# Three fp32r products in place of one fp32 matmul in the attention scores and logits of a hybrid decoder block

## The chip, the cores and the metric

The kernel runs on one core of a Trainium2 chip. A core has a matmul engine (TensorE, PE in the profile, with its weight loads as PEld), VectorE (DVE), ScalarE (ACT), GpSimd (POOL) and SyncE (SP), each with its own instruction queue that is worked off in order, and 16 DMA engines. The metric is device microseconds of one execution; the median of three runs is compared.

## The reference

The block takes x of 512 tokens by 1024 channels in float32. Two branches run in parallel on a normalised h, and an MLP follows.

- `h = rms_norm(x) * (1 + scale1) + shift1`, where scale and shift are products of `silu(c)` with `w_ada`.
- Attention branch: `q_lat` is projected to 8 heads of 64 (`a_q`) and to 4 index heads of 64 (`q_idx`). An index score `sum_h w_idx * relu(q_idx . k_idx)` is made for each query and key; each query keeps the 128 best causal keys, and softmax attention runs over these.
- Recurrent branch: HGRN2, a gated linear recurrence over 4 heads of 128, computed in levels of doubling blocks.
- Both are merged by sigmoid gates, projected and added to x; then a second norm, `square(relu(h2 @ w_mlp1))`, and `w_mlp2`.

The index scores decide which keys are kept, so they are computed with float32 accuracy.

## The kernel before

Everything is transposed, with channels on the 128 partitions and tokens along the free axis. The kernel is one program per engine, written out by hand; engines meet at named semaphores only. Almost all large products are made as three matmuls in fp32r, a float32 format that the array takes in one pass: an operand is split into a `hi` part (a copy to fp32r, made on ScalarE by `split_hi` and its like) and a `lo` part (the float32 value minus `hi`, made on VectorE or GpSimd), and `hi*hi + hi*lo + lo*hi` is summed in PSUM. A plain float32 matmul stands in the trace as two instructions.

The order of work on TensorE is:

1. Start. `x_square` puts squares of x into `x_sq` on ScalarE (seven of eight slices); VectorE (`x_add`) adds them in pairs; TensorE sums four 128x128 blocks of each pair against `ones` into bank 7 (L1650). ScalarE takes the root (`XRS`, L551), VectorE its reciprocal (L1046), and TensorE spreads it over the partitions (`row_spread`). `idle_products(n)` are matmuls whose result nobody reads. VectorE also makes the modulation vector with one dot product of 1024 columns for each slice (`ada_dot1`, L1027).
2. The first projection, `a_pass` (L1662): for each of 8 slices of h, 7 units times three products.
3. The latent q: `lat_hi`, `lat_lo`, the sum of its squares, the index key norm (`KRS`, L588, spread at L1631) and `q_idx` (L1693 to L1695), then v (`values_step`) with the index scores in between: `scores(qb)` at L1731, plain float32, for query blocks 1 to 3 of 128 tokens with 256, 384 and 512 keys. Two heads share a 128-partition tile, so each is a matmul of 64 rows.
4. VectorE finds the 128 best keys by 16 rounds of max-8 and replace; TensorE goes on with the projections of the recurrent branch, and the recurrence itself follows.
5. Attention over four pairs of heads p = 0 to 3. `logits(p, 0, 4)` and `logits(p, 4, 8)` (L1976, plain float32) make 8 tiles of 512, 512, 384, 384, 256, 256, 128 and 128 keys; VectorE masks them (L1347), ScalarE takes the exponential (L804), VectorE divides by the sum (L1356), TensorE transposes (L1989), ScalarE copies the transposes to `prT` (L785), and `values(p)` (L2004) follows. `gate_blocks` of the merge gates fill TensorE's time in between; their results leave on ScalarE by `gate` (L764), and the next unit in the same bank waits for that.
6. The projections, the second norm, and the MLP in two halves: `up` (L1612 to L1614), ScalarE's `up_relu` (L886), `up_square` and `tforms_hi` (L899), and a Strassen-like `quads` (L2187 to L2189).

Of the kernel before, what the change touches and what calls it, by code (L numbers as in the profile page):

```python
# [22 lines left out]
P = 128  # L23
# [36 lines left out]
def hybrid_block(nc, xt, c, cols, ada_t, w_units, out):  # L60
# [17 lines left out]
    with ExitStack() as ctx:  # L78
# [25 lines left out]
        qT = place("qT", RA + 8 * KB, [P, AC, T])  # L104
        score = place("score", RA + 16 * KB, [P, TB, T])
# [14 lines left out]
        qiT = place("qiT", RL + 16 * KB, [P, RC, T])  # L120
# [13 lines left out]
        ada_drop2 = place("ada_drop2", RL + 10 * KB, [P, D])  # L134
# [12 lines left out]
        sig_b = place("sig_b", RL + 16 * KB, [P, KC, T])  # L147
        sq_o = place("sq_o", RA + 16 * KB, [P, 2, T])
# [52 lines left out]
        def sem(name):  # L201
# [13 lines left out]
        xsq_ready, xsq_added, xsq_summed, xroot_ready, xspread = (  # L215
            sem("xsq_ready"), sem("xsq_added"), sem("xsq_summed"), sem("xroot_ready"), sem("xspread"))
        a1_ready, xn_ready, hfull_ready = sem("a1_ready"), sem("xn_ready"), sem("hfull_ready")
        slice_done, a_done = sem("slice_done"), sem("a_done")
        lat_ready, latsq_ready, latsq_added = sem("lat_ready"), sem("latsq_ready"), sem("latsq_added")
        kw_ready, kwsq_ready, k_taken = sem("kw_ready"), sem("kwsq_ready"), sem("k_taken")  # L220
        ki_summed, ki_root, ki_spread, ki_ready = (sem("ki_summed"), sem("ki_root"), sem("ki_spread"),
# [77 lines left out]

        LOGIT_BANK = [[6, 4, 2, 3], [6, 7, 4, 5]]  # L300
# [206 lines left out]
        def _(act):  # L507
# [43 lines left out]
            nc.scalar.activation(XRS, bank[7][:, 0:T:P], ACT.Sqrt, scale=1.0 / D, bias=EPSC  # L551
# [21 lines left out]
            for k in range(RC):  # L573
                act.wait_ge(a_done, k + 1)
                nc.scalar.activation(lat_hi[:, k], bank[k][:], ACT.Identity,
                                     scale=col[:, V_QG + k:V_QG + k + 1])
                nc.scalar.activation(sq[:, k], bank[k][:], ACT.Square).then_inc(latsq_ready, 1)
# [3 lines left out]
            nc.scalar.activation(kw_sq[0:HD, :], bank[2][0:HD, :], ACT.Square).then_inc(kwsq_ready, 1)  # L581
            act.wait_ge(slice_done, 7)
# [8 lines left out]
            for m in range(2):  # L591
                act.wait_ge(qi_done, m + 1)
                nc.scalar.activation(qiT[:, m], bank[SCORE_BANK[m]][:], ACT.Copy).then_inc(qi_taken, 1)
# [4 lines left out]
            split_hi(U_V + 3)  # L598
            nc.scalar.activation(LBC, LBC, ACT.Exp)
# [385 lines left out]
        def _(dve):  # L985
# [14 lines left out]
            def x_add(p):  # L1000

                dve.wait_ge(xsq_ready, [2, 4, 5, 7][p])
                v.tensor_tensor(x_sq[:, 2 * p], x_sq[:, 2 * p], x_sq[:, 2 * p + 1], ALU.add).then_inc(xsq_added, 1)
# [7 lines left out]
            x_add(0)  # L1011
            c_product(0)
            x_add(1)
            c_product(1)
            dve.wait_ge(x_loaded[2], 16)
            step(v.tensor_tensor(x_sq[:, 5], xT[:, 5], xT[:, 5], ALU.mult))
            x_add(2)
            x_add(3)
# [44 lines left out]
            for k in range(RC):  # L1063
                dve.wait_ge(latsq_ready, k + 1)
# [3 lines left out]
            dve.wait_ge(t_lo, KC)  # L1068
            v.tensor_tensor(lat_sq[:], sq[:, 0], sq[:, 1], ALU.add).then_inc(latsq_added, 1)
# [4 lines left out]
            for r in (0, HD):  # L1074
                v.scalar_tensor_tensor(out=kiT[r:r + HD, :], in0=kw[0:HD, :], scalar=KIG, in1=bank[2][0:HD, :],
                                       op0=ALU.mult, op1=ALU.mult).then_inc(ki_ready, 1)
            dve.wait_ge(lat_root, 1)
# [4 lines left out]
                            LRS.unsqueeze(2).to_broadcast([P, TB, IH]), ALU.mult).then_inc(wi_ready, 1)  # L1082

# [228 lines left out]
            def ada_add(i):  # L1312
# [6 lines left out]
                v.tensor_tensor_reduce(out=ada_drop2[:], in0=src[:], in1=c_act[:], scale=1.0,  # L1319
# [4 lines left out]
            def oa_low(j):  # L1324
# [3 lines left out]
                                ALU.subtract).then_inc(oa_ready, 1)  # L1328

            dve.wait_ge(q_ready, 1)  # L1330
            for p in range(PAIRS + 1):
# [5 lines left out]
                if p < PAIRS:  # L1337
# [5 lines left out]
                    for t, qb, e in heads(p):  # L1343
# [6 lines left out]
                            accum_out=smx[:, 1, 2 * p + e, qb:qb + 1]).then_inc(logit_masked, 1)  # L1350
                    for t, qb, e in heads(p):
# [4 lines left out]
                        v.tensor_scalar(w, w, s, None, ALU.mult).then_inc(prob_ready, 1)  # L1356
                    if p == 0:
# [244 lines left out]
        def _(pe):  # L1602
# [53 lines left out]
            idle_products(5)  # L1656
# [33 lines left out]
            for m in range(2):  # L1690
                b = SCORE_BANK[m]
                for i, j in enumerate((m, 2 + m)):
# [30 lines left out]
            def scores(qb):  # L1723
                n = (qb + 1) * P
                for h in range(IH):
                    r = HD * (h % 2)
                    s = nscore[0]
                    nscore[0] += 1
                    if s >= IH:
                        pe.wait_ge(rel_ready, s - IH + 1)  # L1730
                    mm(bank[SCORE_BANK[h]][:, 0:n], qiT[r:r + HD, h // 2, qb * P:(qb + 1) * P], kiT[r:r + HD, 0:n],  # L1731
                       start=True, stop=True).then_inc(score_done, 1)
# [21 lines left out]
            pe.wait_ge(qi_taken, 2)  # L1754
            pe.wait_ge(ki_ready, 2)
# [208 lines left out]
            def logits(p, t0, t1):  # L1964

                for t, qb, e in heads(p)[t0:t1]:
                    i = 8 * p + t
# [298 lines left out]
```

## Time and profile before

| | |
|---|---|
| median of three runs | 771.15 us (770.37 to 771.26) |
| profiled execution, own time | 771.27 us |
| its span, first to last instruction | 769.4 us |
| TensorE busy in the span | 761.0 us (99%) |
| VectorE, ScalarE, GpSimd busy | 630.9, 364.7, 62.7 us |

An instruction's time in the trace includes its way through the engine, so neighbouring matmuls overlap. What a matmul costs a full TensorE is the distance from its start to the start of the next. The profiled execution is 0.12 us above the median.

### The profile page before, as it was taken

How to read it: one execution, taken by the hardware profiler on the slowest of the kernel's cores; microseconds unless marked ns; L12 is line 12 of the kernel's file. 1: busy time of each engine (PE TensorE's matmuls, PEld its weight loads, DVE VectorE, ACT ScalarE, POOL GpSimd, SP SyncE). 2: the span in 40 equal slices, each digit the busy share in tenths (PEclk: the TensorE clock that was granted, in tenths of full speed). 3: DMA queues.
4: the chain of work that ended last, by engine and by line, in shares of the span. 5: the costliest groups of instructions: out<-in, count | busy, mean ns of one | idle time of the engine just before them, and what ended most of it. 6: DMA issues, size and time to landing. Idle time of an engine off the chain costs nothing.

```text
span 769.4 us, 13224 instructions
## 1 busy us (share of the span) xinstructions
PE 761.0 (99%) x5208; PEld 645.8 (84%) x5208; DVE 630.9 (82%) x1129; ACT 364.7 (47%) x577; POOL 62.7 (8%) x64
## 2 busy tenths in 40 slices
PE   7999999999999999999999999999999999999998
PEld 6876878777878777778889988889999888889998
DVE  6975999778998677769966999879998766779996
ACT  5466524455344376654332555654333354454341
POOL 5015344200000000000012000000000000000000
PEclk9999999999999999999999999999999999999999
DMA  9943223221221233345556255312333433213331
GB/s 349 403 140 110 83 83 107 75 67 56 80 86 58 85 107 126 145 142 184 200 180 203 83 165 191 109 55 86 108 110 109 138 110 102 89 55 111 110 110 56
DMA packets 27643, 95.50 MB, mean 124 GB/s; under 512 B 3009, under 2 KB 3393, under 8 KB 27586
## 3 DMA queue, kind: packets, MB, share of 16 engines
q1 hardware_dynamic: 27296, 94.51, 36.8%
q8 instruction: 38, 0.62, 0.3%
q10 hardware_dynamic: 290, 0.20, 0.1%
q14 instruction: 19, 0.16, 0.1%
HBM read 92.61 MB, written 2.10 MB: 123 GB/s over the span
## 4 chain that ended last, share of the span: by engine, by line
PE 94%; DVE 3%; ACT 2%; issue 1%; DMA 1%; DVEq 0%; ACTq 0%
PE bank L1612 10%; PE bank L1614 10%; PE bank L1613 10%; PE bank L2187 7%; PE bank L2189 7%; PE bank L2188 7%; PE bank L1662 5%; PE bank L1841 2%; PE bank L1798 2%; PE bank L1842 2%; PE bank L1843 2%; PE bank L2015 2%; PE bank L1800 2%; PE bank L1799 2%; PE bank L2017 2%; PE bank L2016 2%
## 5 line engine op out<-in xcount | busy, mean ns | idle before, releaser
L1612 PE MATMUL bank<-h_hi,w_hi 128*128 128x512 f32 x328 | 128.2, 391 | 0.6 <-ACT relu_u L886 0.6
L1613 PE MATMUL bank<-h_lo,w_hi 128*128 128x512 f32 x328 | 127.7, 389 | 0.0
L1614 PE MATMUL bank<-h_hi,w_lo 128*128 128x512 f32 x328 | 127.6, 389 | 0.0
L526 ACT ACTIVATE w_hi<-w_raw 128x1024 fp32r<-128x1024 f32 (+2 forms) x94 | 97.4, 1039 | 30.7 <-PE bank L1819 9.4
L1087 DVE TENSOR_TENSOR w_lo<-w_raw,w_hi 128x1024 fp32r<-128x1024 f32 x68 | 83.5, 1236 | 11.7 <-ACT w_hi L526 11.7
L1612 PEld LDWEIGHTS bank<-h_hi,w_hi 128*128 128x128 f32 x328 | 61.6, 188 | 13.4 <-ACT relu_u L886 0.8
L2187 PE MATMUL bank<-u_hi,wf_hi 128*128 128x256 f32 x256 | 72.6, 284 | 0.1
L2189 PE MATMUL bank<-u_hi,wf_lo 128*128 128x256 f32 x256 | 72.4, 283 | 0.0
L2188 PE MATMUL bank<-u_lo,wf_hi 128*128 128x256 f32 x256 | 72.4, 283 | 0.0
L1614 PEld LDWEIGHTS bank<-h_hi,w_lo 128*128 128x128 f32 x328 | 61.6, 188 | 12.9
L1613 PEld LDWEIGHTS bank<-h_lo,w_hi 128*128 128x128 f32 x328 | 61.6, 188 | 12.6
L906 ACT ACTIVATE wf_hi<-w_raw 128x768 fp32r<-128x768 f32 x32 | 26.9, 842 | 54.6 <-PE bank L2189 48.0
L2187 PEld LDWEIGHTS bank<-u_hi,wf_hi 128*128 128x128 f32 x256 | 49.1, 192 | 0.5 <-DVE wf_lo L1513 0.5
L2188 PEld LDWEIGHTS bank<-u_lo,wf_hi 128*128 128x128 f32 x256 | 49.1, 192 | 0.1
L2189 PEld LDWEIGHTS bank<-u_hi,wf_lo 128*128 128x128 f32 x256 | 49.1, 192 | 0.0
L467 POOL TENSOR_TENSOR w_lo<-w_raw,w_hi 128x1024 fp32r<-128x1024 f32 x17 | 41.3, 2430 | 87.3 <-ACT w_hi L526 87.3
L1455 DVE TENSOR_TENSOR sqr_u<-relu_u 128x512 f32<-128x512 f32 x32 | 22.1, 690 | 31.8 <-ACT relu_u L886 31.5
L886 ACT ACTIVATE relu_u<-bank,col 128x512 f32<-128x512 f32 x32 | 21.9, 684 | 44.8 <-PE bank L1614 42.4
L1841 PE MATMUL bank<-h_hi,w_hi 128*128 128x512 f32 x96 | 40.3, 419 | 0.0
L1842 PE MATMUL bank<-h_lo,w_hi 128*128 128x512 f32 x96 | 37.6, 392 | 0.0
L1843 PE MATMUL bank<-h_hi,w_lo 128*128 128x512 f32 x96 | 37.5, 391 | 0.0
L1504 DVE TENSOR_TENSOR wf_lo<-w_raw,wf_hi 128x768 fp32r<-128x768 f32 x32 | 30.5, 954 | 3.9 <-ACT wf_hi L906 3.7
(319 smaller groups left out, 1890.4 us busy)
## 6 DMA issues: line engine op xcount, KB each, us to landing
w_raw<-in_units SPq DMA_DIRECT2D x117, 512.0 KB, 3.3
ada_raw<-in_ada SPq DMA_DIRECT2D x16, 512.0 KB, 10.3
ada_even<-in_ada SPq DMA_DIRECT2D x16, 512.0 KB, 4.5
ada_odd<-in_ada SPq DMA_DIRECT2D x16, 512.0 KB, 4.4
w_raw<-in_units SPq DMA_DIRECT2D x8, 448.0 KB, 10.6
xT<-in_xt SPq DMA_DIRECT2D x4, 512.0 KB, 5.3
out<-xT SPq DMA_DIRECT2D x7, 256.0 KB, 2.5
w_raw<-in_units SPq DMA_DIRECT2D x1, 256.0 KB, 5.1
```

The source lines that it names most:

```text
L467: nc.gpsimd.tensor_tensor(w_lo[:, s], w_raw[:, s], w_hi[:, s].bitcast(F32), ALU.subtract).then_inc(lo_ready, 1)
L526: nc.scalar.activation(w_hi[:, s, 0:width], w_raw[:, s, 0:width], ACT.Copy).then_inc(hi_ready, 1)
L1087: v.tensor_tensor(w_lo[:, n % WS], w_raw[:, n % WS], w_hi[:, n % WS].bitcast(F32), ALU.subtract).then_inc(lo_ready, 1)
L1612: mm(bank[b][:], w_hi[:, slot, j], rhs_hi(i), start=f, stop=False)
L1613: mm(bank[b][:], w_hi[:, slot, j], rhs_lo(i), start=False, stop=False)
L1614: end = mm(bank[b][:], w_lo[:, slot, j], rhs_hi(i), start=False, stop=l)
L1841: mm(bank[b][:], w_hi[:, n % WS, k], h_hi[:, k], start=k == 0, stop=False)
L1842: mm(bank[b][:], w_hi[:, n % WS, k], h_lo[:, k], start=False, stop=False)
L1843: end = mm(bank[b][:], w_lo[:, n % WS, k], h_hi[:, k], start=False, stop=k == KC - 1)
L2187: mm(dst, hi[:, form, w], token_form(t, 0, i), start=f, stop=False)
L2188: mm(dst, hi[:, form, w], token_form(t, 1, i), start=False, stop=False)
L2189: end = mm(dst, lo[:, form, w], token_form(t, 0, i), start=False, stop=l)
```

## The change

It does five things.

- Index scores: `q_idx` and `k_idx` are split into `qi_hi`, `qi_lo`, `ki_hi`, `ki_lo`, and each pair of heads is computed as three fp32r products, the two heads alternating.
- Logits of pairs 1 to 3: ScalarE makes `q_hi` and `k_hi` of a pair (`pair_hi`), VectorE `q_lo` and `k_lo` (`pair_lo`), and `logits` issues three products. Pair 0 stays in float32.
- x sums: TensorE sums each of the eight squared slices by itself with `row_sums` (16 float32 matmuls of 32 tokens each against one column of ones), with idle products in between; VectorE squares slices 5 and 7 and adds nothing; ScalarE's load of the root's table moves ahead of its last square.
- ScalarE's order, first place: the two squares of the latent (L577) move behind `kw` and `kw_sq`.
- ScalarE's order, second place: in the first MLP half, `tforms_hi(0, 0)` moves behind `up_relu(0, 2)`.

The modulation dot products of the second half also write their unused product back over their source.

```diff
-            x_square(7)
-            nc.scalar.activation(warm[:, 2:4], ident[:, 2:4], ACT.Sqrt)
-            act.wait_ge(xsq_summed, KC // 2)
...
+            nc.scalar.activation(warm[:, 2:4], ident[:, 2:4], ACT.Sqrt)
             x_square(6)
+            act.wait_ge(xsq_summed, 1)
...
-                nc.scalar.activation(sq[:, k], bank[k][:], ACT.Square).then_inc(latsq_ready, 1)
...
+            for k in range(RC):
+                act.wait_ge(lat_ready, k + 1)
+                nc.scalar.activation(sq[:, k], bank[k][:], ACT.Square).then_inc(latsq_ready, 1)
...
+            def pair_hi(p):
+                if p == 1:
+                    act.wait_ge(o_done, BH)
+                    act.wait_ge(rt_used, AC)
+                elif p == 2:
+                    act.wait_ge(ob_ready, BH)
+                    act.wait_ge(o_turned, BH)
+                else:
+                    act.wait_ge(logit_done, 8 * (p - 1))
+                nc.scalar.activation(q_hi[p % 2][:], qT[:, p], ACT.Copy).then_inc(qkhi_ready, 1)
+                nc.scalar.activation(k_hi[p % 2][:], kT[:, p], ACT.Copy).then_inc(qkhi_ready, 1)
...
                     gate(KC + 2 * p, sig_b[:, 2 * p])
+                if p == 0:
+                    pair_hi(1)
...
                     gate(KC + 2 * p + 1, sig_b[:, 2 * p + 1])
+                    if 1 <= p < PAIRS - 1:
+                        pair_hi(p + 1)
...
                     up_relu(h, j)
+                    if h == 0 and j == 2:
+                        tforms_hi(0, 0)
                     up_square(h, j)
...
-                    if j % 2 and j < MH - 3:
+                    if j % 2 and j < MH - 3 and (h or j > 1):
                         tforms_hi(h, j // 2)
...
+            for m in range(RC):
+                dve.wait_ge(qi_taken, m + 1)
+                v.tensor_tensor(qi_lo[:, m], bank[SCORE_BANK[m]][:], qi_hi[:, m].bitcast(F32),
+                                ALU.subtract).then_inc(qilo_ready, 1)
             dve.wait_ge(lat_root, 1)
...
+            dve.wait_ge(kihi_ready, 1)
+            v.tensor_tensor(ki_lo[:], kiT[:], ki_hi[:].bitcast(F32), ALU.subtract).then_inc(kilo_ready, 1)
...
+            def pair_lo(p):
+                dve.wait_ge(qkhi_ready, 2 * p - 1)
+                v.tensor_tensor(q_lo[:, p], qT[:, p], q_hi[p % 2][:].bitcast(F32), ALU.subtract
+                                ).then_inc(qklo_ready, 1)
+                dve.wait_ge(qkhi_ready, 2 * p)
+                v.tensor_tensor(k_lo[:, p], kT[:, p], k_hi[p % 2][:].bitcast(F32), ALU.subtract
+                                ).then_inc(qklo_ready, 1)
...
+                    if p == 0:
+                        pair_lo(1)
                     for t, qb, e in heads(p):
                         s = smx[:, 2, 2 * p + e, qb:qb + 1]
...
+                    if 1 <= p < PAIRS - 1:
+                        pair_lo(p + 1)
                     if p == 0:
                         head_out(BH - 1)
...
-            for p in range(KC // 2):
-                pe.wait_ge(xsq_added, p + 1)
-                for b in range(TB):
-                    t = slice(b * P, (b + 1) * P)
-                    end = mm(bank[7][:, t], x_sq[:, 2 * p, t], ones[:], start=p == 0 and b == 0,
-                             stop=p == KC // 2 - 1 and b == TB - 1)
-                end.then_inc(xsq_summed, 1)
+            for s, k in enumerate(X_ACT[:5]):
+                pe.wait_ge(xsq_ready, s + 1)
+                row_sums(7, 0, x_sq[:, k], P, s == 0, False)
+                idle_products(2)
+            pe.wait_ge(xsq_made, 1)
+            row_sums(7, 0, x_sq[:, X_DVE[0]], P, False, False)
+            idle_products(1)
+            pe.wait_ge(xsq_made, 2)
+            row_sums(7, 0, x_sq[:, X_DVE[1]], P, False, False)
+            pe.wait_ge(xsq_ready, len(X_ACT))
+            row_sums(7, 0, x_sq[:, X_ACT[5]], P, False, True).then_inc(xsq_summed, 1)
             idle_products(3)
             pe.wait_ge(xroot_ready, 2)
             row_spread(7, XRS).then_inc(xspread, 1)
-            idle_products(5)
+            idle_products(7)
...
+                    for x, (qi, ki) in enumerate(((qi_hi, ki_hi), (qi_lo, ki_hi), (qi_hi, ki_lo))):
+                        for e in range(2):
+                            r = slice(HD * e, HD * (e + 1))
+                            end = mm(bank[SCORE_BANK[2 * g + e]][:, 0:n], qi[r, g, q], ki[r, 0:n],
+                                     start=x == 0, stop=x == 2)
...
+                if p and t0 == 0:
+                    pe.wait_ge(qklo_ready, 2 * p)
...
+                    for x, (qx, kx) in enumerate(((hi[0], hi[1]), (lo[0], hi[1]), (hi[0], lo[1]))):
+                        for e in range(2):
+                            r = slice(HD * e, HD * (e + 1))
+                            end = mm(bank[LOGIT_BANK[1][t % 4 + e]][:, 0:n], qx[r, q], kx[r, 0:n],
+                                     start=x == 0, stop=x == 2)
```

## Rows read from the trace of the kernel before

**Rows 1.** TensorE's waits: who is waited for, total us, times, longest.
```profile
PE bank L1612 <- ACT relu_u L886: 0.6, 1, 0.6
PE bank L1624 <- ACT kw_sq L581: 0.6, 1, 0.6
```

**Rows 2.** Timeline of the start: start us, duration us, engine, line, operation.
```profile
2.43 3.75 PE L1644 MATMUL bank<-c_row,ones 1*128 1x512 f32 x4 [2.43 <-DMA c_row<-in_c]
6.62 6.51 PE L1650 MATMUL bank<-ones,x_sq 128*128 128x128 f32 x32 [0.45 <-DVE x_sq L1003]
8.91 1.15 ACT L531 ACTIVATE x_sq<-xT 128x512 f32<-128x512 f32 x2 [0.51 <-DMA xT<-in_xt]
13.17 0.26 ACT L551 ACTIVATE sc<-bank,sc 128x4 f32<-128x4 f32 x1 [1.60 <-PE bank L1650]
16.56 1.86 PE L1662 MATMUL bank<-h_hi,w_hi 128*128 128x512 f32 x7 [1.09 <-ACT h_hi L558]
```

**Rows 3.** Windows: L1650 early, L1639 later; length, PE and PEld busy (count), clock, DMA.
```profile
6.60:12.10 5.50, 5.48 (x25) 5.48 (x26) 1.00 1.05 409
...
14.10:15.40 1.30, 1.21 (x10) 1.18 (x10) 1.00 1.04 410
```

**Rows 4.** Timeline of TensorE around one block of 32-token sums.
```profile
97.70 0.39 PE L1613 MATMUL bank<-h_lo,w_hi 128*128 128x512 f32 x1
97.92 0.39 PE L1614 MATMUL bank<-h_hi,w_lo 128*128 128x512 f32 x1
98.24 0.43 PE L1784 MATMUL bank<-twins,q_sq 128*32 128x2 f32 x32
98.61 0.50 PE L1612 MATMUL bank<-h_hi,w_hi 128*128 128x512 f32 x1
```

**Rows 5.** Timeline after the first projection.
```profile
56.26 2.04 ACT L586 ACTIVATE kT<-bank 128x512 f32<-128x512 f32 x4
58.71 0.65 PE L1631 MATMUL bank<-ident,sc 128*128 128x128 f32 x4
```

**Rows 6.** Timeline of the index scores and of VectorE's small step before them.
```profile
60.94 0.94 DVE L1078 SCALAR_TENSOR_TENSOR sc<-sc 128x4 f32<-128x4 f32 x1
65.66 1.13 PE L1731 MATMUL bank<-kiT,qiT 64*128 64x256 f32 x8
74.34 1.99 PE L1731 MATMUL bank<-kiT,qiT 64*128 64x512 f32 x8
76.26 0.50 PE L1746 MATMUL bank<-w_hi,h_hi 128*128 128x512 f32 x1
```

**Rows 7.** Timeline of TensorE, half products of 256 columns in fp32r.
```profile
443.97 0.28 PE L2080 MATMUL bank<-h_hi,w_hi 128*128 128x256 f32 x1
444.09 0.28 PE L2081 MATMUL bank<-h_lo,w_hi 128*128 128x256 f32 x1
```

**Rows 8.** Timeline of TensorE, logits of pair 0.
```profile
268.45 1.77 PE L1976 MATMUL bank<-kT,qT 64*128 64x512 f32 x8
270.15 0.50 PE L1798 MATMUL bank<-h_hi,w_hi 128*128 128x512 f32 x1
...
273.10 0.92 PE L1976 MATMUL bank<-kT,qT 64*128 64x256 f32 x8
```

**Rows 9.** Timeline of pair 0: ScalarE, VectorE and TensorE behind the exponentials.
```profile
277.03 0.60 ACT L764 ACTIVATE sig_b<-bank 128x512 f32<-128x512 f32 x1 [0.45 <-PE bank L1800]
...
277.78 0.47 PE L1798 MATMUL bank<-h_hi,w_hi 128*128 128x512 f32 x1 [0.34 <-ACT sig_b L764]
...
279.93 0.63 ACT L721 ACTIVATE ob_hi<-hg_t 128x512 fp32r<-128x512 f32 x1 [1.35 <-DVE hg_t L1210]
...
280.60 0.69 DVE L1216 TENSOR_TENSOR ob_lo<-hg_t,ob_hi 128x512 fp32r<-128x512 f32 x1 [0.70 <-ACT ob_hi L721]
...
280.83 0.61 PE L1989 MATMUL bank<-ident,pr 128*128 128x128 f32 x4
```

**Rows 10.** Timeline at the start of the MLP's full tiles.
```profile
452.25 0.50 PE L1612 MATMUL bank<-h_hi,w_hi 128*128 128x512 f32 x1 [0.56 <-ACT relu_u L886]
```

More of the change, by code:

```diff
@@ L104, in hybrid_block @@
         qT = place("qT", RA + 8 * KB, [P, AC, T])
+        k_lo = place("k_lo", RA, [P, AC, T], F32R)
+        q_lo = place("q_lo", RA + 8 * KB, [P, AC, T], F32R)
         score = place("score", RA + 16 * KB, [P, TB, T])
@@ L119, in hybrid_block @@
         kiT = place("kiT", RL + 12 * KB, [P, T])
-        qiT = place("qiT", RL + 16 * KB, [P, RC, T])
+        ki_lo = place("ki_lo", RL + 12 * KB, [P, T], F32R)
+        ki_hi = place("ki_hi", RB + 4 * KB, [P, T], F32R)
+        qi_hi = place("qi_hi", RL + 16 * KB, [P, RC, T], F32R)
+        qi_lo = place("qi_lo", RB, [P, RC, T], F32R)
         sq = place("sq", RL + 20 * KB, [P, 2, T])
@@ L147, in hybrid_block @@
         sig_b = place("sig_b", RL + 16 * KB, [P, KC, T])
+        q_hi = [place(f"q_hi{i}", RL + o * KB, [P, T], F32R) for i, o in enumerate((10, 14))]
+        k_hi = [place(f"k_hi{i}", RL + o * KB, [P, T], F32R) for i, o in enumerate((12, 30))]
         sq_o = place("sq_o", RA + 16 * KB, [P, 2, T])
@@ L219, in hybrid_block @@
         lat_ready, latsq_ready, latsq_added = sem("lat_ready"), sem("latsq_ready"), sem("latsq_added")
+        lathi_ready = sem("lathi_ready")
         kw_ready, kwsq_ready, k_taken = sem("kw_ready"), sem("kwsq_ready"), sem("k_taken")
+        qkhi_ready, qklo_ready = sem("qkhi_ready"), sem("qklo_ready")
+        kihi_ready, kilo_ready, qilo_ready = sem("kihi_ready"), sem("kilo_ready"), sem("qilo_ready")
         ki_summed, ki_root, ki_spread, ki_ready = (sem("ki_summed"), sem("ki_root"), sem("ki_spread"),
@@ L546, in _ @@
             x_square(4)
+            nc.scalar.activation(warm[:, 2:4], ident[:, 2:4], ACT.Sqrt)
             x_square(6)
-            x_square(7)
-            nc.scalar.activation(warm[:, 2:4], ident[:, 2:4], ACT.Sqrt)
-            act.wait_ge(xsq_summed, KC // 2)
-            nc.scalar.activation(XRS, bank[7][:, 0:T:P], ACT.Sqrt, scale=1.0 / D, bias=EPSC
+            act.wait_ge(xsq_summed, 1)
+            nc.scalar.activation(XRS, bank[7][:, 0:TB], ACT.Sqrt, scale=1.0 / D, bias=EPSC
                                  ).then_inc(xroot_ready, 1)
@@ L592, in _ @@
                 act.wait_ge(qi_done, m + 1)
-                nc.scalar.activation(qiT[:, m], bank[SCORE_BANK[m]][:], ACT.Copy).then_inc(qi_taken, 1)
+                nc.scalar.activation(qi_hi[:, m], bank[SCORE_BANK[m]][:], ACT.Copy).then_inc(qi_taken, 1)
             act.wait_ge(lb_ready, 1)
@@ L598, in _ @@
             split_hi(U_V + 3)
+            act.wait_ge(ki_ready, 2)
+            nc.scalar.activation(ki_hi[:], kiT[:], ACT.Copy).then_inc(kihi_ready, 1)
             nc.scalar.activation(LBC, LBC, ACT.Exp)
@@ L999, in _, with x_square @@
             v.tensor_tensor(GQK, col[:, V_HQ:V_HQ + 1], col[:, V_HK:V_HK + 1], ALU.mult).then_inc(gqk_ready, 1)
-            def x_add(p):
-                dve.wait_ge(xsq_ready, [2, 4, 5, 7][p])
-                v.tensor_tensor(x_sq[:, 2 * p], x_sq[:, 2 * p], x_sq[:, 2 * p + 1], ALU.add).then_inc(xsq_added, 1)
+            def x_square(k):
+                dve.wait_ge(x_loaded[k // 2], 16)
+                v.tensor_tensor(x_sq[:, k], xT[:, k], xT[:, k], ALU.mult).then_inc(xsq_made, 1)
             def c_product(j):
@@ L1009, in c_product @@
                                 ALU.mult).then_inc(cact_ready, 1)
-            x_add(0)
             c_product(0)
-            x_add(1)
             c_product(1)
[L1015 to L1018, printed above, removed]
+            for k in X_DVE:
+                x_square(k)
             dve.wait_ge(cact_ready, 2)
@@ L1691, in _ @@
                 b = SCORE_BANK[m]
+                if b < RC:
+                    pe.wait_ge(latsq_ready, b + 1)
                 for i, j in enumerate((m, 2 + m)):
@@ L1724, in scores @@
                 n = (qb + 1) * P
-                for h in range(IH):
-                    r = HD * (h % 2)
+                q = slice(qb * P, (qb + 1) * P)
+                for g in range(IH // 2):
                     s = nscore[0]
-                    nscore[0] += 1
+                    nscore[0] += 2
                     if s >= IH:
-                        pe.wait_ge(rel_ready, s - IH + 1)
-                    mm(bank[SCORE_BANK[h]][:, 0:n], qiT[r:r + HD, h // 2, qb * P:(qb + 1) * P], kiT[r:r + HD, 0:n],
-                       start=True, stop=True).then_inc(score_done, 1)
+                        pe.wait_ge(rel_ready, s - IH + 2)
+                    for x, (qi, ki) in enumerate(((qi_hi, ki_hi), (qi_lo, ki_hi), (qi_hi, ki_lo))):
[3 more added lines that the diff above has]
+                                     start=x == 0, stop=x == 2)
+                            if x == 2:
+                                end.then_inc(score_done, 1)
             def values_step(k):
@@ L1753, in _ @@
             values_step(1)
-            pe.wait_ge(qi_taken, 2)
-            pe.wait_ge(ki_ready, 2)
+            pe.wait_ge(qilo_ready, RC)
+            pe.wait_ge(kilo_ready, 1)
             pe.wait_ge(wi_ready, 1)
@@ L1964, in logits @@
             def logits(p, t0, t1):
-                for t, qb, e in heads(p)[t0:t1]:
-                    i = 8 * p + t
+                if p and t0 == 0:
+                    pe.wait_ge(qklo_ready, 2 * p)
+                for t in range(t0, t1, 2) if p else ():
+                    qb = heads(p)[t][1]
+                    q, n = slice(qb * P, (qb + 1) * P), (qb + 1) * P
+                    pe.wait_ge(logit_masked, 8 * p + t - 2)
+                    hi, lo = (q_hi[p % 2], k_hi[p % 2]), (q_lo[:, p], k_lo[:, p])
+                    for x, (qx, kx) in enumerate(((hi[0], hi[1]), (lo[0], hi[1]), (hi[0], lo[1]))):
[3 more added lines that the diff above has]
+                                     start=x == 0, stop=x == 2)
+                            if x == 2:
+                                end.then_inc(logit_done, 1)
+                for t, qb, e in () if p else heads(0)[t0:t1]:
+                    i = t
                     r = HD * e
```

14 lines of the change are left out of this document (8 added, 6 removed).

## The prediction

> **What bounds the kernel now.** I read the page first: TensorE is busy for 99% of the span and carries the chain of waits, so only time that TensorE saves or waits counts. Then TensorE's waits: after the start they come to little more than one microsecond, and two of them, 0.6 us behind `relu_u` and 0.6 us behind `kw_sq`, are at places that the change touches [rows 1]. Then the timeline of five places: the start, the latent, the scores, pair 0, and the entry to the MLP.
>
> At the start the squares are done at 10.06 (8.91 + 1.15), but the 32 matmuls that sum them run from 6.62 to 13.13, and ScalarE's root follows at 13.17; the first real product comes 3.4 us later, at 16.56 [rows 2]. That tail (root, reciprocal, a dot product that VectorE makes in between, spread, scaling) is a chain without a gap, so what the sums gain or lose arrives at 16.56 in full. From there TensorE runs without a pause, so it arrives at the end too. The sums are slow because of the clock: 25 of them fill 5.50 us, 0.22 us each, while ten idle matmuls of the same shape after 14.1 take 1.21 us, 0.12 each [rows 3]. That is the ratio of the two levels, 1.2 and 2.4 GHz. The clock column says 1.00 in both windows; before about 12.2 I trust the durations. TensorE had been pausing 0.45 us ahead of 6.62 [rows 2] and busy from there before it rose.
>
> **The start.** Removed: 32 matmuls, VectorE's four additions, one square on ScalarE. Added: eight blocks of 32 tiny matmuls, eleven idle products between them (behind them three stand as before, and seven in place of five behind the spread, which end ahead of 16.56 at the upper level), and two squares on VectorE. I price a block from one in the middle of full products [rows 4]: from 97.92 to 98.61 is 0.69, less the 0.23 that the full product itself takes, plus 0.11 by which the next product is longer (0.50 against 0.39): 0.57 us. Two of the eight follow another block at once and need no change of shape; 0.3 us for these, from the 0.43 less the way through. An idle product is two instructions, 0.24 us at the upper level and 0.44 at the lower [rows 3]. The trace has no block at the lower level: at least 0.57, at most twice that; I take 0.8 (and 0.5 for the two), since part of it is issue.
>
> TensorE is free for it at 6.2 (2.43 + 3.75) [rows 2]. All at the upper level: 6 x 0.57 + 2 x 0.3 + 11 x 0.24 = 6.7, so 12.9, 0.3 us earlier than 13.13. All at the lower level: 6 x 0.8 + 2 x 0.5 + 11 x 0.44 = 10.6, so 16.8, 3.7 us later. A round of block and two idle products is 1.68 us low and 1.05 high; if the clock rises at 9, 2.8 us have done 1.7 rounds, the other 3.3 take 3.5 and the rest 1.4, so 13.9: 0.8 later. If it rises at 12.2 as now: 15.1, 2.0 later. I take +0.9, a rise a little after 9, because TensorE no longer pauses before 6.62 and so works from 2.43 on; the bounds are -0.3 and +3.7. On ScalarE one square goes and the root's table load moves ahead of the last one. The squares end at 10.06 now, and TensorE comes to that one only after 12, so the load could cost two microseconds before it mattered: nothing.
>
> The Trainium skill (TensorEngine Tiling (Array Packing), Key Properties) says that changing the tiling mode, not just the tile, drains TensorE. The block in [rows 4] agrees: 0.57 us against some 0.26 us of issue. Without drains the six blocks would cost 1.8 us less, and the start would be 0.9 us earlier than before instead of as much later.
>
> **The latent.** `kw_sq` moves up by two operations, so the 0.6 us wait for it [rows 1] goes. But the spread at 58.71 waits for the root that ScalarE makes behind the kT copies, which end at 58.30 [rows 5], and ScalarE does the same operations up to there in another order. The wait moves to 58.71. 0, bounds -0.6 and 0.
>
> **The index scores.** The float32 block of 512 keys takes 1.92 us from 74.34 to 76.26 [rows 6]: four passes of 0.43 (two heads run side by side) and 0.2 for the changes of shape. An fp32r product of 256 columns costs 0.12 [rows 7], one of 512 0.22 to 0.23 (97.70 to 97.92 in [rows 4]). Six steps: 6 x 0.23 + 0.2 = 1.58, 0.34 less. For 384 keys about 0.2 less, since heads 2 and 3 now wait for two ReLUs at once; for 256 keys 6 x 0.12 + 0.2 = 0.92 against 1.06, 0.15 less. Sum -0.7; with no overhead in the products -0.9. I take -0.8. The splits: two `qi_lo`, a little over 0.6 us each like the subtraction of the same size in [rows 9], follow 60.9 on VectorE, so the small step L1078, which took 0.94 us for four columns while GpSimd was working, goes to 62.3 and `ki_lo` comes near 65.3; TensorE wants it at 65.66 [rows 6]. Hidden with 0.3 us to spare; if VectorE is held longer, up to 0.5 lost.
>
> **Logits of pairs 1 to 3.** Now 1.70 us for four tiles of 512 and 384 keys (268.45 to 270.15) and 0.86 for those of 256 and 128 (273.10 on) [rows 8]. New: 3 x (0.23 + 0.175) + 0.2 = 1.42, and 3 x (0.12 + 0.1) + 0.2 = 0.86. So -0.28 each, -0.9 for three pairs. No row shows fp32r at 128 columns: at float32's rate a step is 0.2 instead of 0.1, which gives back 0.3 a pair; with no overhead it is -0.4 a pair. Bounds -1.2 and 0.
>
> **Pair 0.** This is what the added splits cost. `pair_hi(1)` stands on ScalarE behind `gate(KC)` and ahead of the eight exponentials, which run without a gap into `gate(KC + 1)`: two copies of some 0.54 us (0.63 in [rows 9], overlapping). The evacuation at 277.03 had 0.45 us of slack and TensorE waits for it at 277.78, so that comes 0.6 us later. `pair_lo(1)` stands on VectorE ahead of all divisions and of `head_out(3)`, which releases ScalarE's `ob_hi` (279.93), and behind that stand the `prT` copies that free the bank for the transposes at 280.83 [rows 9], with about 0.1 us to spare: two subtractions of 0.69, a little overlapped, make VectorE 1.2 us later, and that gives 1.1 us on TensorE, the 0.6 included. +1.1, bounds +0.6 and +1.4. `pair_hi` and `pair_lo` of pairs 2 and 3 delay only `oa_hi`, the dot products and the weight splits behind these by 1.3 us, and TensorE asks for none of them within that time; nothing.
>
> **The MLP's entry.** `relu_u` of tile 2 stands behind `tforms_hi(0, 0)` in ScalarE's order, and TensorE waited for it until 452.25 [rows 10]. Ahead of `tforms_hi`, which waits for VectorE, it can be made about two microseconds sooner. The wait of 0.56 and the 0.1 of the restart go: -0.7, and TensorE keeps it, as nothing else ends there.
>
> **Sum.** 0.9 + 0 - 0.8 - 0.9 + 1.1 - 0.7 = -0.4. Against the profiled execution's own 771.27 that is 770.9, and its distance of 0.12 to the median puts the forecast at 770.7. Apart from the start the parts give -1.3.
>
> **The rivals.** (A) Slower: the clock stays at its lower level until the idle products behind the sums. For it: idle products are only half of each round, while the dense matmuls from 6.62 needed until 12.2. Then the sums end at 16.8, and the spread queues behind three idle products of 0.44 each, which the root and reciprocal (0.5 us) used to cover: +3.7 + 0.8 = +4.5, total +3.2: 774.3. It decides from a start 2.8 us later on. The Trainium skill (TensorE: Matmul & The Clock Gate, Part 1) says that the throttled clock is the default and sustained activity releases it; it doesn't say whether rounds like these are enough, so it would allow either.
> (B) Faster: the clock is up for nearly all of the sums (-0.3), and the splits at pair 0 hide behind more slack than I see (+0.6): 0.4 less or more from each of the others gives -2.0, 769.1. Against it: the durations show the lower level until 12.2.
> (C) 128 columns go at float32's rate: +0.9, 771.6. Still no change.
> (D) The two heads of an fp32r pair do not run side by side. Each step doubles: 3 x 3 x 0.63 + 6 x 0.53 = +8.8, 779.5. The float32 pairs do, as the 1.70 us show.
>
> **How the numbers follow.** Forecast 0.36, C 0.10, A 0.26, B 0.25, D 0.03. Runs of this kernel lie 0.1% apart, so 0.2% or 1.5 us is what can be told from none. The total is the start's part minus 1.3: faster needs a start no later than 0.2 us earlier, slower one 2.8 later. Faster 0.25 (B), same 0.46, slower 0.29 (A, D). The range 768.9 to 774.3 reaches to B and A; the likeliest case's own is 769.6 to 772.5.
>
> **What would show it.** The distance of the idle products at 6 to 13 us tells the clock; XRS after 13.2 and the first product of `a_pass` after 16.6 tell the start; scores of 1.6 us at 512 keys and logits of 1.4 us the products; a TensorE wait behind `sig_b` of over 0.9 us near 277 and one behind `prT` near 282 pair 0; no wait at the MLP's entry the last. Wrong it would be if the clock rises much sooner or later than at 9 to 12, or if TensorE waits for `ki_lo`.

## The result, and the profile after

The changed kernel takes 775.65 us (median of 5 runs, 775.08 to 775.9) against 771.13 us before (5 runs, 770.37 to 771.26): 4.5 us slower, ratio 1.006 with a 95% interval of 1.0047 to 1.0074. The forecast was 770.7 with a range of 768.9 to 774.3; the result lies above it. The profiled execution took 775.9 us, 774.0 of them its span. The page's busy times, engine by engine:

```profile
PE 766.8 (99%) x5494; PEld 653.5 (84%) x5494; DVE 635.5 (82%) x1135; ACT 367.3 (47%) x583; POOL 62.2 (8%) x64
```

TensorE is as full as before, now for 766.8 us. So the loss is not idle time that a list of waits would show; it must be sought in when the same instruction starts in each trace. This ledger takes matmuls that both kernels have:

| TensorE instruction | before, us | after, us | shift |
|---|---|---|---|
| second matmul of `a_pass`, slice 0 | 16.87 | 22.39 | +5.52 |
| spread of KRS, after the latent | 58.71 | 64.29 | +5.58 |
| first values matmul behind the last scores | 76.26 | 81.40 | +5.14 |
| transposes of pair 0's probabilities | 280.83 | 287.10 | +6.27 |
| gate block behind the first logits of pair 1 | 287.37 | 293.42 | +6.05 |
| the same of pair 2 | 306.08 | 311.86 | +5.78 |
| the same of pair 3 | 324.80 | 330.30 | +5.50 |
| second matmul of the MLP's full tiles | 454.66 | 459.31 | +4.65 |
| last matmul | 766.45 | 771.09 | +4.64 |

The whole loss arises before 22.4 us. Everything behind gives 0.88 us back, with one step the wrong way at pair 0. The timeline of the start (start, duration, engine, line, operation, count), to be held against [rows 2]:

```profile
6.02 0.61 PE L1673 MATMUL bank<-ones,x_sq 128*32 128x1 f32 x32
6.56 1.22 PE L1688 MATMUL bank<-ident,ones 128*128 128x128 f32 x4
7.71 0.61 PE L1673 MATMUL bank<-ones,x_sq 128*32 128x1 f32 x32
...
9.99 0.61 ACT L541 ACTIVATE x_sq<-xT 128x512 f32<-128x512 f32 x1
...
15.71 1.03 PE L1673 MATMUL bank<-ones,x_sq 128*32 128x1 f32 x64
16.68 1.65 PE L1688 MATMUL bank<-ident,ones 128*128 128x128 f32 x6
18.11 1.06 PE L1680 MATMUL bank<-ident,sc 128*128 128x128 f32 x4
18.97 3.19 PE L1688 MATMUL bank<-ident,ones 128*128 128x128 f32 x14
...
20.07 0.81 ACT L567 ACTIVATE h_hi<-tmp,mod,sc 128x512 fp32r<-128x512 f32 x1 [2.15 <-DVE sc L1068]
...
21.82 2.17 PE L1715 MATMUL bank<-h_hi,w_hi 128*128 128x512 f32 x7
```

A round of block and two idle products takes 1.69 us (6.02 to 7.71), in each of the five rounds alike. The fourteen idle matmuls behind the spread take 3.19 us, 0.23 each, where ten took 1.21 in [rows 3]: the pace of 1.2 GHz, to the end of the start. The squares were there at 10.6. In the windows (length, busy time of each engine with its count, clock, DMA):

```profile
6.10:16.70 10.60, 10.60 (x279) 9.15 (x279) 3.91 (x6) 4.47 (x8) 5.90 (x17) 1.00 1.04 406
```

TensorE is busy for all of these 10.60 us (by the profile, which models the ends of matmuls). The clock column's 1.00 is as little use as in [rows 3]: the trace's record of the clock begins only with the rise to 2.4 GHz, here at 22.48 us (at 12.19 in the kernel before), and ahead of it the durations decide.

Behind the start, four waits of TensorE (us in all, times, longest) answer to [rows 1]:

```profile
PE bank L1858 <- ACT sig_b L777: 0.8, 1, 0.8
PE bank L2063 <- ACT prT L798: 0.5, 1, 0.5
PE bank L1680 <- DVE sc L1100: 0.5, 1, 0.5
PE bank L1789 <- ACT rel L647: 0.2, 1, 0.2
```

`kw_sq` and `relu_u` are gone from the list. The spread's wait for VectorE's reciprocal (L1100) and the one for `prT` have come, and that for `sig_b` has grown from the 0.34 of [rows 9]. The timeline of the scores and of the logits of pair 1, against [rows 6] and [rows 8]:

```profile
75.12 0.44 PE L1789 MATMUL bank<-ki_hi,qi_hi 64*128 64x384 f32 x2
...
76.15 0.44 PE L1789 MATMUL bank<-ki_hi,qi_hi 64*128 64x384 f32 x2 [0.25 <-ACT rel L647]
...
76.87 0.50 PE L1806 MATMUL bank<-w_hi,h_hi 128*128 128x512 f32 x1
...
79.81 0.50 PE L1789 MATMUL bank<-ki_hi,qi_hi 64*128 64x512 f32 x2
...
81.40 0.50 PE L1806 MATMUL bank<-w_hi,h_hi 128*128 128x512 f32 x1
...
291.99 0.50 PE L2036 MATMUL bank<-k_hi,q_hi 64*128 64x512 f32 x2
...
293.42 0.50 PE L1858 MATMUL bank<-h_hi,w_hi 128*128 128x512 f32 x1
...
296.82 0.23 PE L2036 MATMUL bank<-k_hi,q_hi 64*128 64x128 f32 x2
296.88 0.28 PE L2036 MATMUL bank<-k_hi,q_lo 64*128 64x128 f32 x2
```

512 keys take 1.59 us (79.81 to 81.40) where they took 1.92, and four tiles of logits 1.43 (291.99 to 293.42) where they took 1.70. The block of 384 keys has gained nothing: it takes 1.75 us (75.12 to 76.87), as its second half starts at 76.15, behind two ReLUs. In the kernel before it took 1.74:

```profile
69.66 1.81 PE L1731 MATMUL bank<-kiT,qiT 64*128 64x384 f32 x8
71.40 0.50 PE L1746 MATMUL bank<-w_hi,h_hi 128*128 128x512 f32 x1
```

A step of two matmuls of 128 columns takes 0.06 us at 296.82 and 0.11 at 296.88.

### The profile page after: what moved, and what is told of

Read it like the earlier page. It is cut to its first block, busy times and chain, and to the rows that moved or that the text cites. A ratio compares the mean times of both kernels' runs of the same rounds, so it can differ in the third digit from the quotient of the medians.

```text
span 774.0 us, 13814 instructions
## 1 busy us (share of the span) xinstructions
PE 766.8 (99%) x5494; PEld 653.5 (84%) x5494; DVE 635.5 (82%) x1135; ACT 367.3 (47%) x583; POOL 62.2 (8%) x64
## 4 chain that ended last, share of the span: by engine, by line
PE 94%; DVE 3%; ACT 1%; issue 1%; DMA 0%; DVEq 0%; ACTq 0%
PE bank L1661 10%; PE bank L1662 10%; PE bank L1663 10%; PE bank L2261 7%; PE bank L2263 7%; PE bank L2262 7%; PE bank L1715 5%; PE bank L1901 2%; PE bank L1902 2%; PE bank L1903 2%; PE bank L2089 2%; PE bank L1858 2%; PE bank L2091 2%; PE bank L2090 2%; PE bank L1860 2%; PE bank L1859 2%
```

## The experiments

**The theory after the result.** TensorE stayed at 1.2 GHz until 22 us, because the rounds of thin blocks and idle products, busy as they are, do not bring the clock up as the dense matmuls did; that is the loss. **The rivals:** the loss lies behind the start; or the start's work is simply too long at any clock.

**1. The old start with the rest of the change.**

```diff
-            for s, k in enumerate(X_ACT[:5]):
-                pe.wait_ge(xsq_ready, s + 1)
-                row_sums(7, 0, x_sq[:, k], P, s == 0, False)
-                idle_products(2)
...
+            for p in range(KC // 2):
+                pe.wait_ge(xsq_added, p + 1)
+                for b in range(TB):
+                    t = slice(b * P, (b + 1) * P)
+                    end = mm(bank[7][:, t], x_sq[:, 2 * p, t], ones[:], start=p == 0 and b == 0,
```

> The changed kernel with the old start: dense sums of x after VectorE's additions, five idle products behind the spread; all else as changed. The clock theory (the start lost 5.5 us, because TensorE stayed at 1.2 GHz until 22.5 us, and the other parts together gained 0.9) expects 0.9 us under the kernel before, about 770.3, with the first real product back at 16.6 and the granted clock at its upper level from about 12.2. The rival (the loss lies in the rest: the fp32r halves cost more than float32, or the splits hold engines up) expects it to stay above the kernel before, by up to 4.5 us.

Measured: 769.92 us, ratio to the kernel before 0.9984 (0.9975 to 0.9993). The first real product is back at 16.64:

```profile
16.64 1.85 PE L1715 MATMUL bank<-h_hi,w_hi 128*128 128x512 f32 x7 [1.09 <-ACT h_hi L567]
```

The rest of the change is a gain of about a microsecond, as the ledger said.

**2. The new start alone on the kernel before** (the same lines the other way round).

> The kernel before with nothing but the new start (blocks of 32 tokens with idle products between them, the two squares on VectorE, the order on ScalarE). The clock theory expects the whole loss here: 5.5 us more than before, about 776.7, the clock up only at 22 to 23 us and the first real product at 21.8. The rival expects it within 1 us of the kernel before.

Measured: 776.8 us, ratio 1.007 (1.0055 to 1.0086). The timeline of its start:

```profile
19.12 2.95 PE L1635 MATMUL bank<-ident,ones 128*128 128x128 f32 x14
21.83 1.86 PE L1662 MATMUL bank<-h_hi,w_hi 128*128 128x512 f32 x7
```

The first real product is at 21.83. The loss is the start's, all of it.

**3. The same idle products, all ahead of the blocks.**

```diff
+            idle_products(11)
             for s, k in enumerate(X_ACT[:5]):
                 pe.wait_ge(xsq_ready, s + 1)
                 row_sums(7, 0, x_sq[:, k], P, s == 0, False)
-                idle_products(2)
```

> The changed kernel with the same eleven idle products and the same eight blocks, but all eleven ahead of the first block, none between. The clock theory (dense 128-column products from about 6.0 us on let the clock rise as they did before, the thin blocks between them do not) expects the upper level near 11.6, the blocks then at some 0.3 us each, the sums done near 14.0 and the first real product near 17.4: about 771.2. The rival (the work itself is too long: 256 thin matmuls, eleven idle products and the changes of tile shape between them) saves only the six changes of shape, 0.27 us each: about 774, with the clock still low at the first real product.

Measured: 776.99 us, ratio 1.0074 (1.0059 to 1.0089): a miss by almost six microseconds. TensorE's timeline says why:

```profile
6.04 5.06 PE L1688 MATMUL bank<-ident,ones 128*128 128x128 f32 x22
11.03 1.98 PE L1673 MATMUL bank<-ones,x_sq 128*32 128x1 f32 x197
17.72 1.02 PE L1673 MATMUL bank<-ones,x_sq 128*32 128x1 f32 x59 [4.71 <-issue]
```

The blocks ran at 0.32 us each (1.98 us for 197 of 256 matmuls), as expected at the upper level. Then TensorE stood still for 4.71 us early in the seventh block, where it waits for no semaphore ("issue"). Here the clock column is of use, since its record begins in time:

```profile
11.70:13.00 1.30, 1.30 (x159) 1.23 (x149) 0.25 (x2) 0.00 (x0) 0.97 (x4) 1.00 1.03 410
...
15.10:16.30 1.20, 0.00 (x0) 0.00 (x0) 0.00 (x0) 0.00 (x0) 0.00 (x0) 0.50 1.04 403
...
17.70:21.90 4.20, 4.18 (x74) 4.16 (x75) 2.05 (x6) 1.10 (x2) 0.00 (x0) 0.52 1.03 408
```

2.4 GHz in the blocks, 1.2 in the later part of the halt (the record has the fall at 14.93) and for four microseconds behind it. And the DMA queues (packets, MB, share) of the window from 15.1 to 16.3 us have a line that no window before it has:

```profile
q8 instruction: 1, 0.02, 5.6%
```

One packet of 0.02 MB on the instruction queue lands inside the halt, while the data queues are full (403 GB/s), and TensorE goes on 1.4 us behind that window. So dense work first does bring the clock up, as the theory had it, and a second thing, which neither theory had, takes the time back.

**4. The idle products between the blocks left out.**

```diff
                 row_sums(7, 0, x_sq[:, k], P, s == 0, False)
-                idle_products(2)
```

> The changed kernel with the eleven idle products between the blocks left out; the three and the seven behind the sums stay. The clock theory: the sums keep pace with the squares and end near 11.2, 5.5 us earlier; behind them the idle products and the spread run densely to about 15.7 or 16, and the clock rises near or a little behind the first real product, which comes at about 16 (h_hi of slice 0 now waits for the first weight slice): the start within 0.5 us of the kernel before, the whole about 770.2. If the clock rises only 5 us after the first real product, another 2 us are lost: 772.5. The rival that the time is that of the blocks alone (0.54 us each and more, at any clock) expects no more than the 11 x 0.43 = 4.7 us of the idle products back at best, and the sums to end later than 12.5.

Measured: 773.29 us, ratio 1.0025 (1.0016 to 1.0035), above both of the theory's numbers (770.2 and 772.5); a halt is part of the reason:

```profile
4.05 3.75 PE L1693 MATMUL bank<-c_row,ones 1*128 1x512 f32 x4 [4.05 <-DMA c_row<-in_c]
7.72 3.43 PE L1673 MATMUL bank<-ones,x_sq 128*32 128x1 f32 x219
15.32 0.70 PE L1673 MATMUL bank<-ones,x_sq 128*32 128x1 f32 x37 [4.17 <-issue]
```

(This execution's row of c came late, at 4.05.) The halt is there again, 4.17 us, and at the same place in the instruction stream: 4 + 219 = 223 matmuls are done, and 4 + 22 + 197 = 223 in experiment 3. That the instructions had not landed is an inference from the equal count and the packet; experiment 9 tests it. The changed kernel's own trace fits it: there the packet lands between 11.8 and 13.0, and the 223rd matmul starts at 15.79, without a halt.

**5. Pair 1's splits later** (on top of experiment 1).

```diff
-                if p == 0:
-                    pair_hi(1)
...
                     gate(KC + 2 * p + 1, sig_b[:, 2 * p + 1])
-                    if 1 <= p < PAIRS - 1:
+                    if p < PAIRS - 1:
                         pair_hi(p + 1)
...
-                    if p == 0:
-                        pair_lo(1)
...
                         head_out_lo(BH - 1)
+                        pair_lo(1)
```

> The changed kernel with the old start, and with pair 1's splits moved: the two copies on ScalarE from ahead of the exponentials to behind the second gate's weight split, the two subtractions on VectorE from ahead of the divisions to behind head 3's last subtraction. Theory (pair 0 costs 1.1 us on TensorE, because the splits stand ahead of work that TensorE waits for): ScalarE had 1.35 us without work at the new place and the copies take some 1.15, so the waits behind sig_b and prT go back to what they were: 1.1 us less than with the old start alone, 768.8. Rival (the fp32r logits themselves or the shared engines cause the waits): no change from 769.9.

Measured: 769.36 us, ratio 0.9972 (0.9962 to 0.9982); 0.6 us under experiment 1 by the medians, where 1.1 were expected, and the intervals overlap, so the medians alone don't settle it. The traces do, for this stretch: the gate block behind pair 1's logits stands at 287.94 with the old start alone and at 286.85 here, by shifts against the kernel before of +0.57 and -0.52, 1.09 apart. ScalarE and TensorE around pair 0, against [rows 9]:

```profile
277.51 0.47 PE L1855 MATMUL bank<-h_hi,w_hi 128*128 128x512 f32 x1 [0.34 <-ACT sig_b L777]
...
278.21 0.62 ACT L816 ACTIVATE q_hi<-qT 128x512 fp32r<-128x512 f32 x1
...
278.73 0.62 ACT L817 ACTIVATE k_hi<-kT 128x512 fp32r<-128x512 f32 x1
...
280.59 0.60 PE L2060 MATMUL bank<-ident,pr 128*128 128x128 f32 x4
```

The wait for `sig_b` is 0.34 again, as in [rows 9], and that for `prT` is gone.

**6. The scores of 384 and 512 keys one values step later** (on top of 5).

```diff
-            scores(2)
             values_step(3)
+            scores(2)
+            values_step(4)
             scores(3)
```

> As the kernel with the later splits, and the scores of 384 and of 512 keys each one values step later. Theory for the index scores that gave 0.44 us instead of 0.8 (the second half of the 384 keys waits 0.42 us for two ReLUs, which wait for VectorE's first product with a weight, 2.2 us while GpSimd works): the wait goes, 0.4 us less, 768.4. Rival (VectorE's selection of the largest scores, now some 3 us later, is waited for somewhere behind): as much slower as it is late, up to 2 us, or no change.

Measured: 768.19 us, ratio 0.9961 (0.9947 to 0.9974). In the timeline the wait is gone; the block of 384 keys takes 1.26 us:

```profile
71.62 0.44 PE L1786 MATMUL bank<-ki_hi,qi_hi 64*128 64x384 f32 x2
...
72.88 0.50 PE L1803 MATMUL bank<-w_hi,h_hi 128*128 128x512 f32 x1
```

By shifts, the stretch from behind the first scores to 189 us gains 0.75 us here and 0.28 in experiment 5: 0.47 from this edit. The rest of the difference between the two medians (0.7 us are its start's, which reached 2.4 GHz earlier: the first real product is at 15.94 here and at 16.64 in experiment 5) is not the edit's.

**7 and 8. Two other starts** (each on top of 5): the last pair's sum as one block behind three dense pairs; and nine idle products, then four blocks on VectorE's pair sums.

```diff
-            for p in range(KC // 2):
+            for p in range(KC // 2 - 1):
...
+            pe.wait_ge(xsq_added, KC // 2)
+            for b in range(TB):
+                for r in range(0, P, 32):
+                    end = mm(bank[7][r:r + 32, b * P:b * P + 1], x_sq[:, KC - 2, b * P + r:b * P + r + 32],
```

> As the kernel with the later splits, but only the last pair of x's squares summed as one block of 32 tokens, behind the three dense pairs. Clock theory: the dense products from 6.6 on let the clock rise near 12.2 as before; the block takes 0.3 to 0.54 us in place of some 1.4 for the eight dense ones; one block is 64 instructions more than none and brings no halt. The sums end near 12.3 instead of 13.1, and the first real product comes 0.8 us earlier: 768.0. Rival (any thin block keeps the clock down): the upper level only well behind the first real product, some 2 us lost: 770.5 or more.

```diff
+            idle_products(9)
             for p in range(KC // 2):
                 pe.wait_ge(xsq_added, p + 1)
+                row_sums(7, 0, x_sq[:, 2 * p], P, p == 0, p == KC // 2 - 1).then_inc(xsq_summed, 1)
```

> As the kernel with the later splits, but nine idle products from about 6.2 us on and then four blocks of 32 tokens, one for each pair that VectorE has added. Clock theory: dense products until about 10.1, so the clock rises late (the rise came 5.6 us behind the first dense product in the kernel before); the blocks end near 12, 1.1 us earlier than the dense sums, but if the rise comes only behind them, between 12 and 17, up to 1 us is given back: 767.7 to 769. The supply theory (blocks back to back outran the instructions): 128 thin matmuls are half of those that ran into the halt, so TensorE stops for less than 1 us or not at all; if it stops for 4 us as with 256 of them, 772.

Measured: 768.49 us (0.9965, 0.9951 to 0.9979) and 767.99 us (0.9965, 0.9953 to 0.9977). The second's timeline:

```profile
6.03 3.66 PE L1689 MATMUL bank<-ident,ones 128*128 128x128 f32 x18
9.62 1.00 PE L1674 MATMUL bank<-ones,x_sq 128*32 128x1 f32 x96
...
15.05 1.85 PE L1709 MATMUL bank<-h_hi,w_hi 128*128 128x512 f32 x7 [1.08 <-ACT h_hi L567]
```

Three blocks take 1.00 us, no halt comes, and the first real product is at 15.05, 1.5 us ahead of [rows 2]; in experiment 7 it is at 15.32. So a few thin blocks behind dense matmuls don't keep the clock down: the rival of 7 falls. How much of the gain is theirs is not shown: both intervals overlap that of experiment 5, and in these two traces the clock rose early, at 10.06 and 8.96.

**9. The sums as 32 matmuls of 128 tokens and one column** (on top of the changed kernel; eleven idle products first, as in 3).

```diff
+            idle_products(11)
...
+            for k in range(KC):
+                for b in range(TB):
+                    end = mm(bank[7][:, b:b + 1], x_sq[:, k, b * P:(b + 1) * P], ones[:, 0:1],
```

> The changed kernel with eleven idle products ahead of the sums, as in the run where TensorE halted for 4.7 us, but each square summed by four matmuls of 128 tokens and one column instead of sixteen-fold four of 32: 32 matmuls (64 instructions with their weight loads) in place of 256 (512). Supply theory (TensorE halted because its next instructions, 16 KB in one packet on the instruction queue, had not landed): no halt, the clock up near 11.6, the sums done between 13.5 and 16 (0.07 to 0.15 us each), and the first real product between 17 and 19: 771 to 773. Rival (a one-column matmul itself, or the squares, makes TensorE stop): a halt of some 4 us again, 775 or more.

Measured: 780.82 us, ratio 1.0129 (1.0112 to 1.0146). (The float32 form makes two instructions of each, so 64 appear.) TensorE's timeline and the windows:

```profile
10.49 11.27 PE L1700 MATMUL bank<-ones,x_sq 128*128 128x1 f32 x64
...
26.75 1.97 PE L1712 MATMUL bank<-h_hi,w_hi 128*128 128x512 f32 x7
```

```profile
11.00:16.00 5.00, 5.00 (x35) 5.00 (x35) 0.72 (x2) 0.00 (x0) 1.69 (x5) 0.73 1.03 410
16.00:20.00 4.00, 4.00 (x21) 4.00 (x20) 0.00 (x0) 0.00 (x0) 0.00 (x0) 0.50 1.02 408
20.00:25.00 5.00, 5.00 (x25) 5.00 (x25) 2.21 (x6) 1.10 (x2) 0.00 (x0) 0.50 0.97 361
```

No halt, so the squares and one-column matmuls as such don't stop TensorE, and the supply theory stands on this side. The time was badly missed, for the first theory's own reason: the matmuls ran at 0.11 us until 13.3 and at 0.21 from there, the clock column goes from 0.73 to 0.50, and TensorE is busy for 5.00 of 5.00 us. The clock had been up and fell while TensorE had nothing but one-column matmuls to do, and was still down at the first real product.

**10. Five idle products in a round in place of two** (on the changed kernel).

```diff
-                idle_products(2)
+                idle_products(5)
```

> The changed kernel with five idle products in place of two behind each of the first five blocks: 15 idle products more. If the work alone set the time of the start, they would add 15 x 0.43 = 6.4 us: about 782. Clock theory (it is the rounds' half idle work that left the clock at 1.2 GHz): with these rounds the clock rises inside the sums, near 12 as with unbroken dense products; then the later rounds take 1.7 us instead of 2.7, the sums end near 18.2 and the first real product comes at about 21, no later than in the changed kernel in spite of 15 more products: about 774.5 to 776.

Measured: 776.75 us, ratio 1.0078 (1.0059 to 1.0096): 1.1 us more than the changed kernel, for 6.4 us of added work. The timeline:

```profile
12.52 2.51 PE L1688 MATMUL bank<-ident,ones 128*128 128x128 f32 x10
...
15.50 1.83 PE L1688 MATMUL bank<-ident,ones 128*128 128x128 f32 x10
17.26 0.43 PE L1673 MATMUL bank<-ones,x_sq 128*32 128x1 f32 x32
17.62 1.38 PE L1688 MATMUL bank<-ident,ones 128*128 128x128 f32 x10
18.94 0.43 PE L1673 MATMUL bank<-ones,x_sq 128*32 128x1 f32 x32
```

Ten idle matmuls take 2.51 us, then 1.83, then 1.38: the clock rose inside the sums, behind 15.5 and ahead of 17.6 (by the record at 16.47), six microseconds earlier than with two. The theory's direction is right, its time (near 12) was too early. The time itself is a looser witness: the four runs spread from 775.54 to 778.95, and the profiled one (777.73) has its first real product at 23.88, 2.1 us behind the changed kernel's.

These rows also answer the rival that the work is too long at any clock. At the upper level a round of block and five idle products takes 1.68 us (17.26 to 18.94); the ten idle matmuls are 1.1 of it, so a block with its changes of shape costs 0.56, the prediction's 0.57. By the prediction's sum at that price, an estimate, the changed kernel's sums would have ended at 12.9 with the clock up.

**11. All that held together:** 5, 6 and the start of 8.

> All that held together: the fp32r halves for scores and logits, the MLP entry's order, pair 1's splits later, the scores of 384 and 512 keys one values step later, and the start with nine idle products and four blocks of 32 tokens on VectorE's pair sums. If the gains add up: from 768.0 (the four blocks) less the 0.5 us that the later scores gave in their trace: 767.5, about 3.7 us under the kernel before. Rival: the earlier start moves the scores against GpSimd's work and the 0.5 us does not come: 768.0.

Measured: 767.23 us, ratio 0.9962 (0.9949 to 0.9976), 3.5 us under the 770.73 of the kernel before on that chip. The interval overlaps those of 6, 7 and 8, so that the parts add up in full is not shown by it.

## Why the prediction was wrong

- **The start: the step that failed.** "I take +0.9, a rise a little after 9, because TensorE no longer pauses before 6.62 and so works from 2.43 on" took any work for the work that raises the clock. The rise came at 22.48, and the start cost +5.52. The sum for "all at the lower level" was good: sums at 16.8, and the idle products behind them begin at 16.68; the 0.8 us for a block at that level, a guess between two bounds, gave rounds of 1.68, and they took 1.69, which is partly luck. What failed was the choice between the ends, and then the upper end itself: the bound of +3.7 and rival A's +4.5 stop at the spread. Behind it the seven idle products, priced as ending "ahead of 16.56 at the upper level", took 3.19 us and held TensorE until 21.82, though `h_hi` was there at 20.88: 0.8 us more. The first real matmuls at 1.2 GHz cost another 0.3.
- **Rival A** named the mechanism and gave it 0.26. Its argument, that idle products are only half of each round, was in hand; experiments 2, 3 and 10 bear it out. Its price was 1.0 us short, for the reason just given.
- **The changes of shape and the clock.** Two idle products are four matmuls of 0.22 us at the lower level [rows 3], 0.88, and a round has 1.15 for them and the change back to thin blocks (6.56 to 7.71). The 0.3 us left agree with the drain at a change of the tiling mode that the Trainium skill names (TensorEngine Tiling (Array Packing), Key Properties); no run here takes it apart. TensorE was busy for 10.60 of 10.60 us in the rounds by the profile, and the clock stayed down. The Trainium skill (TensorE: Matmul & The Clock Gate, Part 1) has sustained activity release it; this trace doesn't agree, if a busy engine is taken for that.
- **The latent:** 0 predicted, +0.06 measured; the wait moved to the spread's 0.5 us as described.
- **The index scores:** -0.8 predicted, -0.44 measured. 512 keys gave -0.33 (-0.34 predicted), 256 keys -0.16 (-0.15). The term that was mis-sized is 384 keys: -0.2 predicted, nothing measured, because the two ReLUs that its second half waits for cost 0.42 of its time. Experiment 6 takes that wait away and gets 0.47 back. `ki_lo` was not waited for.
- **Logits of pairs 1 to 3:** -0.9 predicted, -0.77 measured. **Rival C** falls: steps of 128 columns took 0.06 and 0.11 us, not 0.2. **Rival D** falls too: the twelve matmuls of 512 keys fill 1.59 us, and one after another at 0.23 they would need 2.8.
- **Pair 0:** +1.1 predicted, +1.13 measured, with both waits at the places named; experiment 5 removes it by moving the splits.
- **The MLP's entry:** -0.7 predicted, -0.85 measured; no wait is left there.

So all but the start comes to -0.88 where -1.3 was forecast, and the start decided.

## What to carry to other kernels

Before thinning out TensorE's work at the start of a kernel, ask what that work did for the clock: here a TensorE that the profile shows as busy was not enough, and what is saved in matmuls can be paid twice, in the rounds themselves and in the idle products and first real ones behind them. A split that is added to an engine's order costs what stands behind it in that order and is waited for, and moving it a few places can give that back whole. Count the instructions too where a kernel starts with the DMA queues full: 256 thin matmuls back to back cost a halt of over four microseconds here, though that late instructions were its cause is inferred.

## What the runs showed that was not expected

- TensorE halted for 4.71 and 4.17 us with no semaphore to wait for, both times after 223 matmuls, when 256 thin ones stood back to back in the first 18 us. A packet on the instruction queue landed inside the halt. With 128 of them (experiment 8), or with the same squares in 32 matmuls (experiment 9), there was none. The changed kernel has the same 256, spread over ten microseconds, and didn't halt.
- The clock fell from 2.4 to 1.2 GHz at 13.3 us in experiment 9 while TensorE was busy without a pause, with one-column matmuls.
- When the clock rises varies from run to run: dense matmuls began at 6.62 in [rows 2] and 2.4 GHz came at 12.2; in experiment 8 they began at 6.03 and the thin blocks from 9.62 on already ran at the upper level. Experiments 3 and 9 begin with the same eleven idle products, at 6.04 and 6.03, and the clock rose at 11.52 and at 9.90. Some of the spread of a microsecond between runs of one kernel will be this; that was not measured by itself.
- VectorE's first product with a weight took 2.23 us for 256 columns while GpSimd was splitting weights, and 0.42 for 384 columns when it was not; the ReLUs behind it are what the 384 keys wait for.
